# Six ada products leave the attention for the waits at norms 3, 5, 6, 7 and the pool layer, in one PSUM bank held from the first ffn on

## The reference, cut to what matters

```python
x = first_block(x, p, ...)      # mixers, out projection, conv ffn, gated embedding (w_ple_gate)
x = second_block(x, c, ...)

def second_block(x, c, ada_w, ada_b, ...):
    cond = silu(c)                                   # 1 x 1024
    for layer in range(2):
        mod = cond @ ada_w[layer] + ada_b[layer]     # 1024 x 6144: the "ada products"
        sh1, sc1, g1, sh2, sc2, g2 = split(mod, 6)
        h = rms_norm(x, norm1_g[layer]) * (1 + sc1) + sh1
        if layer == 0:
            y = pool_mixer(h, pool_w_in, pool_w_grp, pool_scale, pool_w_out)
        else:
            kv = (norm and modulation of x with kv_ada_w) @ w_kv
            y = dilated_attention(h, kv, attn_w_q, attn_w_o)
        x = x + g1 * y
        h = rms_norm(x, norm2_g[layer]) * (1 + sc2) + sh2
        x = x + g2 * conv_ffn(h, ffn_w_up, ffn_conv_w, ffn_conv_b, ffn_w_down)
    return rms_norm(x, final_g)
```

## Time and profile before

| | |
|---|---|
| median of 3 runs | 1352.49 us (1351.99 to 1353.58) |
| the profiled execution's own time | 1351.78 us |
| its span | 1349.8 us |
| mean granted TensorE clock | 0.965 |
| TensorE matmul busy | 1284.6 us (95%) |
| GpSimd, ScalarE, VectorE busy | 849.4, 621.9, 565.1 us (63, 46, 42%) |
| bytes moved by DMA | 242.82 MB, mean 180 GB/s |

### The profile page before, as it was taken

One profiled execution on the slowest core, in us unless ns is written; L12 is line 12 of the kernel. 1 busy time (PEld: TensorE's weight loads), 2 busy tenths in 40 slices (PEclk: granted clock), 3 DMA queues, 4 the chain that ended last, 5 costly groups with the idle time before them and its releaser, 6 DMA issues.

```text
span 1349.8 us, 25787 instructions
## 1 busy us (share of the span) xinstructions
PE 1284.6 (95%) x10737; PEld 1196.6 (89%) x10737; DVE 565.1 (42%) x1275; ACT 621.9 (46%) x962; POOL 849.4 (63%) x441
## 2 busy tenths in 40 slices
PE   7997989889999999898999999999999999999998
PEld 6983447779899999898999999999998888999998
DVE  6658676642676671523433303132222224433301
ACT  5540442125665553654544434554534454544442
POOL 8984400025788877555778776846655655887772
PEclk8997979989999999899999999999999999999999
DMA  8759985603455555425455555453647793455550
GB/s 265 203 183 348 330 294 190 216 32 103 161 178 185 180 180 194 134 94 188 151 180 180 164 191 167 141 157 94 188 128 254 244 296 100 152 187 188 172 172 32
DMA packets 232817, 242.82 MB, mean 180 GB/s; under 512 B 9068, under 2 KB 201726, under 8 KB 232702
## 3 DMA queue, kind: packets, MB, share of 16 engines
q1 hardware_dynamic: 232382, 241.08, 54.7%
q10 hardware_dynamic: 320, 0.10, 0.0%
HBM read 240.11 MB, written 1.05 MB: 179 GB/s over the span
## 4 chain that ended last, share of the span: by engine, by line
PE 89%; DVE 5%; ACT 2%; issue 2%; POOL 0%; ACTq 0%; DVEq 0%
PE banks L548 87%; DVE arena L1686 2%; PE banks L1332 1%; DVE arena L1693 1%; DVE banks L1693 1%; PE banks L558 1%; ACT arena L2426 0%; DVE banks L1686 0%; ACT ring_hi L2426 0%; DVE arena L1897 0%; ACT hn_hi L2426 0%; ACTq L1435 0%; PE banks L861 0%; ACT hn L2426 0%; PE banks L984 0%
## 5 line engine op out<-in xcount | busy, mean ns | idle before, releaser
L1613 POOL TENSOR_TENSOR ring_lo<-ring,ring_hi 128x2048 fp32r<-128x2048 f32 (+1 forms) x176 | 719.0, 4098 | 431.1 <-ACT ring_hi L2426 430.8
L548 PE MATMUL banks<-hn_hi,ring_lo 128*128 128x256 f32 (+1 forms) x1864 | 524.7, 286 | 0.0
L548 PE MATMUL banks<-hn_hi,ring_hi 128*128 128x256 f32 x1696 | 483.5, 289 | 12.1 <-ACT hn_hi L2426 11.3
L548 PE MATMUL banks<-hn_lo,ring_hi 128*128 128x256 f32 x1696 | 446.5, 283 | 0.0
L2426 ACT ACTIVATE ring_hi<-ring 128x2048 fp32r<-128x2048 f32 (+1 forms) x176 | 299.7, 1705 | 170.7 <-PE banks L548 127.2
L548 PEld LDWEIGHTS banks<-hn_hi,ring_lo 128*128 128x128 f32 (+1 forms) x1864 | 363.0, 195 | 0.1
L548 PEld LDWEIGHTS banks<-hn_hi,ring_hi 128*128 128x128 f32 x1696 | 332.8, 196 | 15.6 <-issue 9.4
L548 PEld LDWEIGHTS banks<-hn_lo,ring_hi 128*128 128x128 f32 x1696 | 311.2, 192 | 0.1
L2426 ACT ACTIVATE arena<-banks 128x256 f32<-128x256 f32 (+6 forms) x238 | 92.8, 410 | 249.4 <-PE banks L548 173.9
L548 PEld LDWEIGHTS banks<-arena 64*128 64x128 f32 (+4 forms) x1282 | 119.3, 182 | 66.7 <-issue 43.0
L548 PE MATMUL banks<-arena 128*64 128x128 f32 (+9 forms) x1282 | 148.0, 309 | 24.6 <-DVE arena L1686 9.8
(11 more groups left out here) (263 smaller groups left out, 1582.3 us busy)
## 6 DMA issues: line engine op xcount, KB each, us to landing
ring<-in_ada_w_dram SPq DMA_DIRECT2D x48, 1024.0 KB, 8.2
ring<-in_ffn_w_up_dram SPq DMA_DIRECT2D x44, 1024.0 KB, 5.2
ring<-in_w_up_dram SPq DMA_DIRECT2D x22, 1024.0 KB, 5.1
ring<-in_ffn_w_down_dram SPq DMA_DIRECT2D x16, 1024.0 KB, 4.9
ring<-in_w_kv_dram SPq DMA_DIRECT2D x15, 1024.0 KB, 5.5
ring<-in_w_in_dram SPq DMA_DIRECT2D x9, 1024.0 KB, 8.5
ring<-in_w_kv_dram SPq DMA_DIRECT2D x18, 512.0 KB, 3.9
ring<-in_attn_w_q_dram SPq DMA_DIRECT2D x18, 512.0 KB, 3.8
```

The lines of the kernel that those rows point to most:

```text
L548: return nc.tensor.matmul(o, l, r, start=start, stop=stop, **k)
L1613: led.emit(g.tensor_tensor(low, raw, high.bitcast(F32), ALU.subtract), sem("lo_ready"))
```

## The change

The six late ada products are issued at other places: one at norm 3 behind the spread; two at norm 5, one ahead of the mean square and one behind the spread; one in the pool layer between `grouped(3)` and `pooled(3)`; one at norm 6 and one at norm 7, both behind the spread. They no longer use bank 7 but a bank that is taken out of the rotation by `held_back` in the first ffn's down phase and goes back with the last product at norm 7. `ada_columns` stands at turn 2 of the attention, `late_pad` is filled ahead of the first ffn, and `late_pad` and `late_sums` get other places in SBUF. The arithmetic is the same.

```diff
             def last_tile(job, key, x, ms):
...
                 close(last)
+                if ms[0] == 5:
+                    ada()
                 mean_square_of(ms[0], b_ms, ms[1], (0, 6, 7))
                 if ms[0] != 1:
                     spread(ms[0])
+                if ms[0] in (5, 6):
+                    ada()
...
-            ada_used = [0]
+            ada_used, late_bank = [0], [None]
...
+                        home = late_bank[0] if late_one else ADA_BANK
                         if first:
                             pe.wait_ge(sem("pad_ready") if late_one else sem("cond_ready"), 1)
-                            emptied(ADA_BANK)
-                            ada_open[0] = True
+                            if not late_one:
+                                emptied(ADA_BANK)
+                                ada_open[0] = True
...
                         if final:
                             close(last)
-                            ada_open[0] = False
+                            if late_one:
+                                held.remove(home)
+                            else:
+                                ada_open[0] = False
...
                     if f == 0 and m == 3:
                         spread(4, False)
+                    if f == m == 0:
+                        late_bank[0] = held_back()
+                        ada_left.extend(LATE_ADA)
...
                 if f < 2:
                     mean_square_of(ms[0], b_ms, ms[1], (0, 6, 7))
                     spread(ms[0])
+                    ada()
...
             grouped(3)
+            ada()
             pooled(3)
...
-                if 6 < i < 13:
-                    ada()
-                if i == 13:
+                if i == 2:
                     ada_columns(True)
...
+            led.emit(v.memset(late_pad, 0.0))
+            settle()
+            ts(late_pad[:, :, 7], cond[:, :], 0.5, MUL, signal=sem("pad_ready"))
             ffn(0)
```

More of the change, by code:

```diff
@@ L233, in two_block_kernel @@
         dk, dv, dq = at(0, 2, 6, T), at(3072, 2, 2, 3, T), at(6144, 2, 6, T)
-        late_sums = at(0, 512)
+        late_sums = at(13824, 512)
         dsc = [shaped(late[:, 6 * T:9 * T], 2, 3 * P), at(9216, 2, 6 * P)]
@@ L240, in two_block_kernel @@
         hn2_lo, hn2_hi = parts("hn2_lo", 14400, KT, T), parts("hn2_hi", 16448, KT, T)
-        assert 18496 + 39 * KT <= 18808 and 18808 + 3 * P <= HI0
-        late_pad = at(18496, KT, 39)
+        assert 13312 + FT * T <= 18944 and 18944 + 39 * KT <= HI0 and 18808 + 3 * P <= HI0
+        late_pad = at(18944, KT, 39)
         outt = at(0, 2, D)
@@ L690, in ada @@
                         first, final = i == group[0], i == group[-1]
+                        home = late_bank[0] if late_one else ADA_BANK
                         if first:
                             pe.wait_ge(sem("pad_ready") if late_one else sem("cond_ready"), 1)
-                            emptied(ADA_BANK)
-                            ada_open[0] = True
+                            if not late_one:
+                                emptied(ADA_BANK)
+                                ada_open[0] = True
                         if final:
-                            numbered(("adas", late_one), ADA_BANK)
+                            numbered(("adas", late_one), home)
                         for k in range(KT):
@@ L702, in ada @@
                             x = late_pad[:, k, 7 - row:39 - row] if late_one else cond_pad[:, k, 31 - i:63 - i]
-                            last = mm(banks[q:q + 32, ADA_BANK, :], x, w[:, k % 4, :],
+                            last = mm(banks[q:q + 32, home, :], x, w[:, k % 4, :],
                                       start=(first and k < 4), stop=(final and k >= 4), tile_position=(0, q),
@@ L1369, in _ @@
                     queries(0, br, i)
-            ada_left.extend(LATE_ADA)
             coming = itertools.chain(projections(1), projections(2), projections(3))
@@ L2383, in dil_out @@
                 tt(y, b[:, 0:P], y, MUL, *freed(("dy", i)))
-            led.emit(v.memset(late_pad, 0.0))
-            settle()
-            ts(late_pad[:, :, 7], cond[:, :], 0.5, MUL, signal=sem("pad_ready"))
             dil_bias(0)
```

## The result

The changed kernel takes 1394.96 us (median of 4 runs, 1393.37 to 1396.62) against 1352.24 us (also 4 runs): 1.0315 times the kernel before, with a 95% interval of 1.03 to 1.0331. It is 3.15% slower. The forecast was 1382 us with a range up to 1394. The direction and the chains at the four norms came as told; the loss was 13 us larger, just outside the range, and the gain told for the attention was about half real.

What follows compares the result with a forecast made beforehand. TensorE, busy 95% of the span, was taken to bound the kernel. Attention -12.5, the four norms +40.6 and the pool layer +1 gave +29.1 on 1351.78: 1380.9, shifted to the runs' median, 1382 us; range 1365 to 1394.

Steps and rivals of the forecast that it cites:

- The bank: Behind norms 3, 5, 6, 7: first matmul waits for VectorE's eighth low part, losing 7.97 and three times 5.86, together 25.5 us.
- The ring: Later-issued weights delay norms 3, 6 and 7 by 3.3, 1.2 and 2.9 us, and norm 5's first matmul by 13.4.
- Sum of the four: Norms 3, 5, 6 and 7: first matmuls later by 11.3, 13.4, 7.1 and 8.8 us, together 40.6.
- Gain 12.5 us: Attention: removing six ada products saves 11.2 us, and the 1.30 us wait ahead of the sums' columns goes.
- VectorE's fill ... nothing: Ahead of the first ffn: filling the padded condition lies under a TensorE stage with VectorE 42% busy, costing nothing.
- The pool layer, +1 taken: Pool layer: later landings and seven banks against a 1.88 us gap filled by the sixth product: +1 us, between -1 and +5.
- The 1.4 to 2.5 us of each stay: zero: First four tiles behind norms 3, 5, 6, 7: still start at 1.2 GHz, so their clock loss is unchanged.
- Hiding: Norms 3, 5, 6, 7: five products fit idle time in holes of 4 to 7 us, costing nothing; 9.3 if none hidden.
- A: Norms 3, 5, 6, 7 lose nothing: 1341 us, or 1333 if products keep the clock at 2.4 GHz; chance 0.05.
- B: Norms 3, 5, 6, 7: weights land in time, only the 25.5 us overlap is lost: 1366.5 us; chance 0.13.
- C: Norms 3, 5, 6, 7: weights land later still, at the 8.2 us of ada chunks: 1393.8 us; chance 0.1.

Runs made afterwards that it cites:

- the bank alone: Kernel before, with only a PSUM bank held out of rotation from the first ffn's down phase to norm 7, no product moved: 1377.95 us.
- the run without loads: Changed kernel, with the six products multiplying a constant in SBUF, so their twelve weight chunks are not loaded: 1367.21 us.
- high part held: Changed kernel, with ScalarE writing the third weight chunk's high part after the norm's own work at norms 3, 6 and 7: 1382.94 us.
- the single product at norm 5: Changed kernel, with one ada product at norm 5 instead of two, the freed one at attention turn 12, columns at turn 13: 1384.78 us.
- both moves of products between turns: Changed kernel, pool layer's product to attention turn 12, columns to 13: 1388.53 us; kernel before, six products in turns 1 to 6, columns at 7: 1357.85 us.
- the version with halves: Changed kernel with three first tiles, held high part, moved fill, products halved around the spread at norms 3, 6, 7: 1351.43 us; also at norm 5: 1347.58 us.

## Why the forecast was off

**The bank: right.** 25.5 us were worked out from VectorE's last low parts; the bank alone cost 24.8 in the median (27.7 in the holes of its profiled execution), and the holes of the run without loads grew by 26.0.

**The ring: right in kind, 3.7 us too small.** "Sum of the four: 11.3 + 13.4 + 7.1 + 8.8 = 40.6" measured 12.5 + 14.1 + 7.3 + 10.4 = 44.3. At norms 3 and 7, where ScalarE stood longest, I moved only the root and took the matmuls of mean square and spread at the pace of before; they ran at 1.2 GHz after a wait of 2.8 us and more. These two norms make 2.8 of the 3.7. The high part held and the single product at norm 5 show that the rest is as I put it.

**"Gain 12.5 us" in the attention: wrong, 6.6.** The step read "with no wait ahead of it: this is work on the path". No wait stood ahead, but the product at turn 12 and the wait ahead of the columns lay over a chain of ScalarE and GpSimd that ends at turn 13. Taken away, 3.44 us of it became a wait, and the waits of the whole attention grew from 3.8 to 6.1 us where they were to shrink by 1.3. That is 3.6 of the 5.9 us missed, and both moves of products between turns confirm it. I had asked what releases the product and not what comes due behind it. The other 2.3 are the clock, as TensorE's busy time fell by 8.9 us and not by 11.2: 1.0 in the first four tiles behind norm 7 (13.93 and not 12.92), the rest behind the new wait. With the clock up behind that wait (high part held) the attention gave back 10.0. This is the largest miss, and no bound of the range had a smaller gain in the attention. The total lies 1 us above the range, so the smaller misses share in it.

**"VectorE's fill ... nothing": wrong, 3.3.** The work was 0.2 us, and the place was under a GpSimd instruction that held it for 3.7, with the first ffn's tiles queued behind on VectorE: 1.8 us of waiting for TensorE and 1.5 at a lower clock behind it.

**The pool layer, +1 taken, 3.1 measured.** It lay inside the bounds. The out projection's chunks took 5.8 us to land in the median (5.0 before), ScalarE stood 5.43 us for one of them, and TensorE waited 1.70 us for the rows behind it.

**The rest.** The four misses are 3.7 + 5.9 + 3.3 + 2.1 = 15.0. The stages that the sum left out were 1.9 shorter and the start 0.7 later, which gives the 13.6 between 29.1 and 42.7. "The 1.4 to 2.5 us of each stay: zero" held for the four groups together (54.1 and 53.9), though each moved by 0.8 to 1.0; what the sum had no term for is the clock behind waits elsewhere.

**Hiding: right about idle time, wrong about its size.** "Their own price is nothing as long as the hole stays" held only because the bank's wait covered it. With that wait gone, a product behind the spread costs what it wins in the attention: 1352.4 us for three of them.

**Rivals.** A (norms lose nothing) fell. Its remark that a product in the hole might keep the clock up failed in the changed kernel (54.1 us for the four groups) and came true only in the version with halves. B (the bank alone, 1366.5) fell; with C (1393.8) the total nearly agrees and the cause does not: the pool layer's chunks landed in 5.0 us in the median, not 8.2.

## What to carry to other kernels

A bank taken out of a rotation that fits exactly costs a whole overlap at every place where the next user falls on a bank that comes free late: count the banks that are opened ahead of a stage's first instruction. Work is moved into a wait only if it fits the part of the wait where it is put, at the clock that holds there; in halves around the spread it did, in one piece behind it it did not. Before work is taken off the bounding engine, look at what becomes due behind it: one of the attention's six products was cover for another engine's chain. And a new wait is priced with what the clock does behind it: the same wait of 3.44 us came with a granted clock of 0.50 in the six us behind it in one run and of 1.00 in another, which made the attention 2.7 us longer or not.

## What was not expected of the hardware

A VectorE instruction of 128x8 with SBUF operands alone took 3.88 us (tensor_scalar) and 3.86 us (scalar_tensor_tensor) while GpSimd wrote a weight part of 4.6 us, and 0.18 us where GpSimd was idle; the memset just ahead of it took 0.32 us in both places. An ada product took 1.92 us in the attention and 3.41 us at norm 3 behind a wait of 2.76 us, with a granted clock of 0.55; put ahead of the spread and behind it with no such wait before, its halves took 1.06 and 1.07 us at a clock of 1.00. After a wait of 3.44 us TensorE ran 28 matmuls in six us at a clock of 0.50 in one run and 50 at 1.00 in another; a wait of 2.2 us at the first ffn's start was followed by 0.57 in one and by 1.00 in another. What decides between the two no run here shows.
